# Expert rows in a two-block transformer kernel: one-hot products on TensorE, or a scratch tensor and indirect DMAs on GpSimd

## The reference

```python
def swiglu(x, wg, wu, wd):
    return (jax.nn.silu(x @ wg) * (x @ wu)) @ wd

def moe_swiglu(xn, router, wg, wu, wd):
    t = xn.reshape(B * S, D)                      # 256 x 1024
    logits = (t @ router).astype(jnp.float32)     # 256 x 8
    top_val, top_idx = lax.top_k(logits, TOP_K)   # TOP_K = 2
    gates = jax.nn.softmax(top_val, axis=-1)
    combine = jnp.sum(jax.nn.one_hot(top_idx, N_EXPERTS, dtype=jnp.float32) * gates[..., None], axis=1)
    out = jnp.zeros_like(t)
    for e in range(N_EXPERTS):                    # 8 experts, inner width 3584
        out = out + combine[:, e:e + 1].astype(t.dtype) * swiglu(t, wg[e], wu[e], wd[e])
    return out.reshape(B, S, D)
```

## Time and profile before

| | us |
|---|---|
| median of 3 runs | 2555.48 (2554.43 to 2555.93) |
| the profiled execution | 2555.27 |
| its span (first to last instruction) | 2554.0 |
| PE busy | 2469.2 (97%) |
| DVE busy | 1804.5 (71%) |
| ACT busy | 1522.6 (60%) |
| GpSimd busy | 0.2 |

### The profile page before, as it was taken

The page is one execution under the profiler, slowest core; times in us unless marked ns, Lnnn a source line. Parts: engine busy times, 40 slices in busy tenths (PEclk is TensorE's granted clock), DMA queues, the critical chain, the costliest instruction groups (busy, mean ns, idle before and its releaser), DMA issues.

```text
span 2554.0 us, 29811 instructions
## 1 busy us (share of the span) xinstructions
PE 2469.2 (97%) x11806; PEld 2042.7 (80%) x11806; DVE 1804.5 (71%) x2291; ACT 1522.6 (60%) x1970; POOL 0.2 (0%) x4
## 2 busy tenths in 40 slices
PE   8999999999999998899999889999999999999997
PEld 7888788788878887688887678888888888888885
DVE  5655655566566556654465669989899999998995
ACT  5445544544455446644456567777777777777774
POOL 0000000000000000000000000000000000000000
PEclk9999999999999999899999889999999999999999
DMA  8453555545445554345455269999999999999981
GB/s 280 143 168 130 166 183 186 174 149 165 149 145 193 190 169 149 99 153 184 162 182 165 88 244 346 373 334 366 342 366 343 362 339 359 354 351 354 347 316 75
DMA packets 263484, 596.54 MB, mean 234 GB/s; under 512 B 11846, under 2 KB 16812, under 8 KB 263340
## 3 DMA queue, kind: packets, MB, share of 16 engines
q1 hardware_dynamic: 263324, 594.57, 67.0%
q10 hardware_dynamic: 16, 0.00, 0.0%
HBM read 593.48 MB, written 1.05 MB: 233 GB/s over the span
## 4 chain that ended last, share of the span: by engine, by line
PE 88%; DVE 6%; ACT 4%; issue 1%; DMA 0%; SPq 0%; ACTq 0%; DVEq 0%
PE PS L573 26%; PE PS L575 26%; PE PS L574 26%; DVE WL L1798 2%; PE PS L1022 1%; ACT WH L1313 1%; PE PS L1073 1%; PE PS L633 1%; PE PS L678 1%; PE PS L1059 1%; PE PS L762 1%; PE PS L748 1%; PE PS L642 1%; PE PS L717 1%; ACT AR L1579 0%
## 5 line engine op out<-in xcount | busy, mean ns | idle before, releaser
L1798 DVE TENSOR_TENSOR WL<-raw,WH 128x1024 fp32r<-128x1024 f32 (+2 forms) x798 | 931.6, 1211 | 327.7 <-ACT WH L1313 323.4
L1313 ACT CAST WH<-raw 128x1024 fp32r<-128x1024 f32 (+2 forms) x798 | 790.6, 1041 | 317.7 <-PE PS L575 316.3
L573 PE MATMUL PS<-WH,XTH 128*128 128x512 f32 (+2 forms) x2368 | 949.5, 401 | 19.7 <-DVE XTL L1807 7.0
L575 PE MATMUL PS<-WH,XTL 128*128 128x512 f32 (+2 forms) x2368 | 922.2, 389 | 0.0
L574 PE MATMUL PS<-WL,XTH 128*128 128x512 f32 (+2 forms) x2368 | 920.6, 389 | 0.0
L573 PEld LDWEIGHTS PS<-WH,XTH 128*128 128x128 f32 x2368 | 447.9, 189 | 116.0 <-issue 16.6
L575 PEld LDWEIGHTS PS<-WH,XTL 128*128 128x128 f32 x2368 | 447.1, 189 | 93.5
L574 PEld LDWEIGHTS PS<-WL,XTH 128*128 128x128 f32 x2368 | 448.5, 189 | 87.6 <-issue 3.4
L1798 DVE TENSOR_TENSOR WL<-AR,WH 128x1024 fp32r<-128x1024 f32 x332 | 390.3, 1221 | 24.3 <-ACT WH L1313 23.5
L1313 ACT CAST WH<-AR 128x1024 fp32r<-128x1024 f32 x332 | 332.3, 1051 | 71.0 <-PE PS L575 71.0
L573 PE MATMUL PS<-WH,HTH 128*128 128x512 f32 x792 | 315.4, 398 | 5.9 <-DVE HTL L1977 4.5
(11 more groups left out here) (300 smaller groups left out, 1495.3 us busy)
## 6 DMA issues: line engine op xcount, KB each, us to landing
raw<-in_w_in SPq DMA_DIRECT2D x92, 1024.0 KB, 5.2
raw<-in_moe_w_gate SPq DMA_DIRECT2D x57, 1024.0 KB, 7.0
raw<-in_moe_w_up SPq DMA_DIRECT2D x57, 1024.0 KB, 6.8
AR<-in_moe_w_down SPq DMA_DIRECT2D x56, 1024.0 KB, 7.1
raw<-in_moe_w_down SPq DMA_DIRECT2D x56, 1024.0 KB, 7.0
AR<-in_moe_w_gate SPq DMA_DIRECT2D x55, 1024.0 KB, 6.6
AR<-in_moe_w_up SPq DMA_DIRECT2D x55, 1024.0 KB, 6.9
raw<-in_w_up SPq DMA_DIRECT2D x32, 1024.0 KB, 5.5
```

The lines of the kernel that those rows point to most:

```text
L573: pe.matmul(o, lh, rh, start=start, stop=False, skip_group_check=True)
L575: return pe.matmul(o, ll, rh, start=False, stop=stop, skip_group_check=True)
L1313: act.copy(WH[:, i % WR, c], slots[s][:, c]).then_inc(*wh.inc(i, h))
L1798: dve.tensor_tensor(WL[:, i % WR, c], slots[s][:, c], WH[:, i % WR, c].bitcast(F32), ALU.subtract).then_inc(*wl.inc(i, h))
```

## The change

The token rows of experts 1 to 7 no longer come by one-hot products, and the results of experts 0 to 6 no longer go back by them. Expert 0's gather and expert 7's scatter stay as they are.

- A new instruction stream on GpSimd fills a DRAM scratch tensor `expert_rows` (8 x 128 rows) with zeros while the first layer runs; ACT and DVE wait for that before they write the area again in layer 1.
- DVE works out, for each token and each of its two choices, the row number expert x 128 + slot (`places`), and GpSimd writes the token's row of XN there with four indirect DMAs (two halves of the tokens, two choices).
- For each expert e from 1 on, GpSimd waits until the result of expert e-2 is in YE, writes it to a second scratch tensor `expert_sums`, and loads the 128 rows of expert e into YE. PE waits for that (d_in) and transposes the eight blocks of YE, in place of 16 products.
- PCM, its transposes, PTM and the four products with the additions are left only for expert 7. In its groups 3 and 5 DVE runs `unfold`: for each half of the tokens, X plus weight times row, for two rows that GpSimd has gathered from `expert_sums` into YB (an area set to zero first, since rows out of bounds, those of expert 7, are not fetched).

```diff
+        YB = ar(2560, 2048).rearrange("p (c n) -> p c n", c=2)
+        ZERO = ar(0, 1024)
+        IDX = [sb(f"IDX{c}", [P, T], U32) for c in range(2)]
+        rows_dr = nc.dram_tensor("expert_rows", (NE * P, D), F32, kind="Internal").ap()
+        sums_dr = nc.dram_tensor("expert_sums", ((NE - 1) * P, D), F32, kind="Internal").ap()
...
+        def gpsimd():
+            pool = nc.gpsimd
+            pool.wait_ge(*xadd.at("o1", 0, 1, 1))
+            pool.memset(ZERO, 0.0).then_inc(*zeroed.inc(0))
+            pool.wait_ge(*zeroed.at(0))
+            for e in range(NE):
+                pool.dma_start(rows_dr[e * P:e * P + P, :], ZERO).then_inc(d_zero, 16)
+            pool.wait_ge(d_zero, 16 * NE)
+            pool.wait_ge(*xnm.at(0))
+            pool.wait_ge(*place.at(0))
+            for t in range(T):
+                for c in range(2):
+                    pool.indirect_dma_start(rows_dr, bass.IndirectOffsetOnAxis(ap=IDX[c][:, t:t + 1], axis=0), XN[:, t, :], None,
+                                            bounds_check=NE * P - 1, oob_is_err=False).then_inc(d_rows, 16)
+            pool.wait_ge(d_rows, 64)
+            for e in range(1, NE):
+                if e > 1:
+                    pool.wait_ge(*ya.at(e - 2))
+                    pool.wait_ge(*yd.at(e - 2))
+                    pool.dma_start(sums_dr[(e - 2) * P:(e - 1) * P, :], YE).then_inc(d_out, 16)
+                    pool.wait_ge(d_out, 16 * (e - 1))
+                pool.dma_start(YE, rows_dr[e * P:e * P + P, :]).then_inc(d_in, 16)
+                pool.wait_ge(d_in, 16 * e)
+            pool.wait_ge(*ya.at(NE - 2))
+            pool.wait_ge(*yd.at(NE - 2))
+            pool.dma_start(sums_dr[(NE - 2) * P:(NE - 1) * P, :], YE).then_inc(d_out, 16)
+            for t in range(T):
+                if t:
+                    pool.wait_ge(*fold.at(t - 1))
+                pool.memset(ar(2560, 2048), 0.0).then_inc(*zeroed.inc(1 + t))
+                pool.wait_ge(*zeroed.at(1 + t))
+                if t == 0:
+                    pool.wait_ge(d_out, 16 * (NE - 1))
+                for c in range(2):
+                    pool.indirect_dma_start(YB[:, c, :], None, sums_dr, bass.IndirectOffsetOnAxis(ap=IDX[c][:, t:t + 1], axis=0),
+                                            bounds_check=(NE - 1) * P - 1, oob_is_err=False).then_inc(d_back[t], 16)
...
                 def prep(e):                       # tensor()
-                            for t in range(T):
-                                m = pe.matmul(PS[:, bk, c * P:c * P + P], XN[:, t, cc * P:cc * P + P], GPM[:, b, t, :],
+                            if e:
+                                m = pe.transpose(PS[:, bk, c * P:c * P + P], YE[:, cc * P:cc * P + P], ident)
+                            for t in range(0 if e else T):
+                                m = pe.matmul(PS[:, bk, c * P:c * P + P], XN[:, t, cc * P:cc * P + P], GPM[:, t, :],
                                               start=t == 0, stop=t == 1)
...
                 def put_back(e):                   # tensor(), and the same on DVE
-                    for t in range(T):
+                    for t in range(T if e == NE - 1 else 0):
...
+                        if (l, g) == (1, 4):       # scalar() and vector(), ahead of the copy into QT
+                            act.wait_ge(d_zero, 16 * NE)
...
+                def places():                      # vector()
+                    for c, one in enumerate((o1, oh)):
+                        at, far, sl = te(sm[:, 136:152]), sm[:, 88 + 4 * c:90 + 4 * c], sm[:, 96 + 4 * c:98 + 4 * c]
+                        dve.tensor_tensor(at, one, te(SLOT), ALU.mult).then_inc(*own.inc())
+                        dve.wait_ge(*own.now())
+                        dve.tensor_reduce(sl, at, AX.X, ALU.add).then_inc(*own.inc())
+                        dve.wait_ge(*own.now())
+                        dve.tensor_scalar(far, sl, float(P), 4096.0, ALU.is_ge, ALU.mult)
+                        dve.scalar_tensor_tensor(out=sl, in0=f8[:, :, c], scalar=float(P), in1=sl, op0=ALU.mult, op1=ALU.add).then_inc(*own.inc())
+                        dve.wait_ge(*own.now())
+                        dve.tensor_tensor(sl, sl, far, ALU.add).then_inc(*own.inc())
+                        dve.wait_ge(*own.now())
+                        m = dve.tensor_copy(IDX[c][:, :], sl)
+                    m.then_inc(*place.inc(0))
+
+                def unfold(t):
+                    dve.wait_ge(d_back[t], 32)
+                    for c, w in enumerate((w1, w2)):
+                        m = dve.scalar_tensor_tensor(out=X[:, t, :], in0=YB[:, c, :], scalar=w[:, t:t + 1], in1=X[:, t, :],
+                                                     op0=ALU.mult, op1=ALU.add)
+                        if c == 0:
+                            m.then_inc(*own.inc())
+                            dve.wait_ge(*own.now())
+                    m.then_inc(*fold.inc(t))
...
                 def prep(e):                       # vector()
-                    select(e, GPM[:, b], PCM[:, b], SLOT, gsel.inc(e))
+                    if e == 0:
+                        select(e, GPM, None, SLOT, gsel.inc(e))
+                        places()
+                    if e == NE - 1:
+                        select(e, None, PCM, SLOT, gsel.inc(e))
...
+                        if e == NE - 1 and n in (3, 5):
+                            unfold(n // 2 - 1)
```

More of the change, by code:

```diff
@@ L337, in program @@
         LT = AR[0:8, 1536:1792]
-        GPM = ar(0, 512).rearrange("p (b t j) -> p b t j", b=2, t=2)
-        PCM = ar(512, 512).rearrange("p (b t j) -> p b t j", b=2, t=2)
-        PTM = ar(1024, 512).rearrange("p (b m) -> p b m", b=2)
+        GPM = ar(0, 256).rearrange("p (t j) -> p t j", t=2)
+        PCM = ar(256, 256).rearrange("p (t j) -> p t j", t=2)
+        PTM = ar(512, 256)
         YE = ar(1536, 1024)
+        YB = ar(2560, 2048).rearrange("p (c n) -> p c n", c=2)
[3 more added lines that the diff above has]
+        sums_dr = nc.dram_tensor("expert_sums", ((NE - 1) * P, D), F32, kind="Internal").ap()
         HX = ar(15360, 1024).rearrange("p (b n) -> p b n", b=2)
@@ L466, in program @@
         lgt, sel, gd, cnt = (route_v.part(x) for x in ("lgt", "sel", "gd", "cnt"))
+        place = sig("place", 1)
+        zeroed, fold = sig("zeroed", 3), sig("fold", 2)
+        d_zero, d_rows, d_in, d_out = (sem(x) for x in ("d_zero", "d_rows", "d_in", "d_out"))
+        d_back = [sem(f"d_back{t}") for t in range(T)]
         xnm, ge = route_a.part("xnm"), route_a.part("ge")
-        gsel, gx, xgh, xgl, ptt, ptm = sig("gsel", NE), sig("gx", NE, 2), sig("xgh", NE, 2), sig("xgl", NE, 2), sig("ptt", NE), sig("ptm", NE)
+        gsel, gx, xgh, xgl, ptt, ptm = (sig("gsel", (0, NE - 1)), sig("gx", NE, 2), sig("xgh", NE, 2), sig("xgl", NE, 2),
+                                        sig("ptt", (NE - 1,)), sig("ptm", (NE - 1,)))
         es, hm, et, eth, etl = (sig(x, NG1) for x in ("es", "hm", "et", "eth", "etl"))
-        ya, yd, scm, sx, xfin = sig("ya", NE), sig("yd", NE), sig("scm", NE, 2, 2), sig("sx", NE, 2, 2), sig("xfin", 1)
+        ya, yd, scm, sx, xfin = (sig("ya", NE), sig("yd", NE), sig("scm", (NE - 1,), 2, 2), sig("sx", (NE - 1,), 2, 2),
+                                 sig("xfin", 1))
         FN = FE // 512
@@ L1010, in prep @@
                 def prep(e):
-                    b = e % 2
                     yield
                     for hf, bk in enumerate((7, 3)):
-                        if hf == 0:
+                        if (e, hf) == (0, 0):
                             pe.wait_ge(*gsel.at(e))
-                        if (e, hf) == (0, 0):
                             pe.wait_ge(*xnm.at(0))
+                        elif hf == 0:
+                            pe.wait_ge(d_in, 16 * e)
                         bank(bk)
@@ L1028, in prep @@
                         yield
-                    bank(7)
-                    for t in range(T):
[L1031 to L1034, removed]
+                    if e == NE - 1:
+                        bank(7)
+                        pe.wait_ge(*gsel.at(e))
+                        for t in range(T):
+                            m = pe.transpose(PS[:, 7, t * P:t * P + P], PCM[:, t, :], ident)
+                        m.then_inc(*ptt.inc(e))
+                        free[7] = ptm.at(e)
+                        yield
                 def up1(kind, e, n, bk, fresh):
@@ L1072, in put_back @@
                             bank(2 + j)
-                            pe.matmul(PS[:, 2 + j, :], PTM[:, e % 2, t * P:t * P + P], YE[:, j * 512:j * 512 + 512],
+                            pe.matmul(PS[:, 2 + j, :], PTM[:, t * P:t * P + P], YE[:, j * 512:j * 512 + 512],
                                       start=True, stop=True).then_inc(*scm.inc(e, t, j))
@@ L1661, in put_back @@
                     act.copy(YE[:, 0:512], PS[:, 0, :]).then_inc(*ya.inc(e))
-                    for _ in range(6):
+                    for _ in range(6 if e == NE - 1 else 2):
```

(13 more changed lines are left out.)

16 lines of the change are left out of this document (11 added, 5 removed).

## The result

| | before | after |
|---|---|---|
| median | 2555.39 us (4 runs, 2554.43 to 2555.93) | 2508.99 us (4 runs, 2507.52 to 2510.78) |
| ratio to before | | 0.9819, 95% interval 0.9807 to 0.9832 |
| profiled execution, span | 2555.27, 2554.0 us | 2507.52, 2506.2 us |

The kernel is 46.4 us faster, 1.8%. The prediction was 2511 us, a gain of 44 us.

A forecast was written before the change was run, and what follows sets the result against it. The prediction took PE (TensorE) to set the pace in the expert stage. Terms removed from PE summed to 45.0 us, less 1 for unfold: 44 us off the median of 2555.48, giving 2511 us, range 2505 to 2542.

The forecast's parts named there:

- PE sets the pace: Expert stage: a TensorE microsecond taken out of the expert loop is a microsecond of time, unless something else reaches 100%.
- Scatter products and PCM's transposes: PE's queue: 28 scatter products at 0.87 us removed, 24.3 us; PCM's transposes for experts 0 to 6, 1.6 us.
- Gather products: PE's queue, 7 experts: each half of eight products (1.79 us) becomes four transposes (0.45 us), 18.7 us off.
- The fourth rival: PE's gather: a transpose costs what a gather half costs, 18.7 us less gain, 2530 us; chance 0.04.
- The period: Time per expert in the expert stage: falls from 125.1 us by 3.5, 2.7 and 0.2 to 118.7 us.
- my count of matmuls: PE's work in one period before the change: 124.7 of 125.1 us accounted for, 0.4 us left open.
- The select at the start: Start of expert stage: PE waits for four DVE operations, of which two stay; 0.4 us off.
- The row chain: PE's wait for d_in: write and load, 14 to 18 us, fit in 28 us per expert; cost 0.
- The transfers: Expert stage: 45.09 MB per expert in 118.7 us, 380 GB/s, can be carried; 386 GB/s was seen in one window.
- the bound by lead and volume: Expert stage: with 18 us of lead, transfers bind only if seven experts' bytes need over 849 us, below 372 GB/s.
- The first and the third rival: Transfers bind softly at 365 GB/s, 2527 us, chance 0.13; or hard at about 354 GB/s, 2553 us, chance 0.05.
- unfold, 1 us of 0 to 5: DVE's queue, twice in the last expert: 2.6 us in one piece against a 3.0 us cushion; cost taken as 1 us.

## Why the prediction was right

- *PE sets the pace.* Right. PE is busy in every window before and after, and each half of the change is worth its place in PE's queue.
- *Scatter products and PCM's transposes, 24.3 + 1.6 us.* The run that keeps them has +26.8 us in its stage, +27.1 in its median.
- *Gather products, 18.7 us.* The run that keeps them has +18.6 in the stage, +19.4 in the median. The fourth rival falls with it.
- *The period, 118.7 us.* It is 118.55, 6.56 less than before, where the places add up to 6.4. The 0.16 left are a part of the 0.4 us per period that my count of matmuls had left open, and they go with the scatter: its half is 3.88 us in a period (122.43 less 118.55) against 3.7 priced, the gather's 2.66 against 2.7. Which instruction takes them is open.
- *The select at the start, 0.4 us.* PE's wait for it has gone from 1.97 us to 1.46. Right, and places() is hidden: DVE still waits 3.15 us for ACT behind it.
- *The row chain is hidden.* Right. I took 7 us for a transfer on the rows of a quiet 512 KB and a loaded 1024 KB; write and load take 6 to 7 each. An indirect scatter occupies GpSimd for 1.0 us. The reserve is 13 to 15 us. The zeroing is hidden too: its eight writes are issued from 303.23 us on and have landed by 321.0, over 240 us before they are needed.
- *The transfers.* Right, and with more room than I could know: the bound by lead and volume was 372 GB/s, and the runs carry 390 over a period and 394 at the ceiling. The first and the third rival fall. They were not idle rivals, since 4.2 MB more per expert undo the whole gain. The Trainium skill, "DMA: Bandwidth & Descriptors", section "Where 436 GB/s comes from", has the HBM side bind at about 358 GB/s; the measurement decides, and here that figure is over 30 GB/s too low.
- *DVE.* 109.3 us in a period, predicted 109.4. That it fits to the tenth is luck: the 3.8 us taken off are the additions and selects alone, and the copy of PTM, which goes too, has 0.4 us of its own in the trace of before; busy times overlap at their ends.
- *unfold, 1 us of 0 to 5.* It costs 0; 2.6 us fit in a cushion of 2.9, with 0.3 to spare. This term was over-sized, by 1 us.
- *The sum.* The select's 0.4 us stand ahead of the stage, so 43.6 of the 44 are to be found in it. It lost 45.6, 2.0 more: 1 us from unfold, about 1 from the 0.16 in each period. The other 0.8 us between stage and medians are within the spread of the runs.

## What to carry to other kernels

Where an engine is never idle, price a removed instruction by the starts of its neighbours, not by its duration: 0.87 us for a product whose two records say 0.59 each. The three terms priced so gave 44.6 us, where the stage lost 45.6. Before moving such work to transfers, count two reserves and not only the mean rate, the microseconds between when the data is there and when it is asked for, and the bytes that a lead of prefetched pieces can lend; both could be read from the trace before. Keep GpSimd to issuing: 24 copies of SBUF data per expert beside two-input DVE work cost 75 us, more than the change gained. A stall costs more than its length: 14.8 us of waiting brought 2 us more behind it, while the clock was at its lower level.

## What the runs showed of the hardware

- Transfers of one core carry 390 GB/s over a period of 118.6 us with nothing waiting for them, and 394 over 96 us when they are behind (DMA share 1.04). A copy from DRAM to DRAM counts little more than once.
- A 128x1024 float32 copy on GpSimd (1.05 us at its shortest) and a DVE subtraction with two SBUF inputs (1.22 us) hold each other up: 1.92 and 2.05 us side by side. DMA issues on GpSimd, direct (0.54 us) or indirect (1.0 to 2.0 us), do not lengthen the subtraction (1.23 us at the longest of 625).
- After stalls of 14 to 15 us PE's matmuls start at the pace of 1.2 GHz, 0.43 us apart, in one case until 3.0 us after the stall's end; six such stalls cost 1.3 to 2.7 us each beyond their length. Of two gaps of 2.3 us, one was followed by 4 us at a granted clock of 0.57 and the other by none.
